# Hybrid decoder step on one core: the first head's operands turned inside the projection stage, the prompt's cross attention with the values held stationary, the last output tile half by half

## What is computed

```python
q = (_rms_norm(c_q, q_norm_g) @ w_uq).reshape(b, s, MLA_HEADS, NOPE_DIM + ROPE_DIM)
...
y_mla = _mla_prompt(q_lat, q_rope, c_kv, k_r, w_uv[l])          # 8 heads, causal, 1024 keys
mem_k, mem_v = _mem_kv(mem_prompt, w_mk[l], w_mv[l])            # 256 memory tokens
y_x = _cross_attention(q_x, mem_k, mem_v)                       # 4 heads of width 128
...
m = (g[:, :, 0] * ((y_mla * silu(z_mla)) @ w_p_mla) + ...)      # three gated branches
return _layer_norm(DEEPNORM_ALPHA * h + m @ w_o, ln_g, ln_b)
```

## Time and profile before

| | |
|---|---|
| median of 3 runs | 1564.25 us (1562.61 to 1572.33) |
| the profiled execution: own time, span | 1564.4 us, 1562.6 us |
| PE busy, share of the span | 1510.5 us, 97% |
| PEld busy | 1344.2 us, 86% |
| DVE, ACT, POOL busy | 663.3, 441.7, 411.4 us |
| mean granted clock of the tensor engine | 0.986 |

### The profile page before, as it was taken

One profiled execution on the slowest core, in us unless ns is written; L12 is line 12 of the kernel. 1 busy time (PEld: TensorE's weight loads), 2 busy tenths in 40 slices (PEclk: granted clock), 3 DMA queues, 4 the chain that ended last, 5 costly groups with the idle time before them and its releaser, 6 DMA issues.

```text
span 1562.6 us, 26122 instructions
## 1 busy us (share of the span) xinstructions
PE 1510.5 (97%) x10008; PEld 1344.2 (86%) x10008; DVE 663.3 (42%) x1451; ACT 441.7 (28%) x1066; POOL 411.4 (26%) x295
## 2 busy tenths in 40 slices
PE   7999999999999999978999999999999999999997
PEld 7998877775677777755999999999999999999885
DVE  3252367763533333334343452224533354019653
ACT  4223356661454444423111111111111121114100
POOL 3110057773023222101222222221222222226112
PEclk9999979999999999998999999999999999999998
DMA  5441020002643559447211211111121111113321
GB/s 208 142 190 33 4 78 1 1 1 75 176 122 106 157 165 236 138 143 253 49 41 41 54 42 41 47 49 41 41 54 42 47 40 49 41 42 108 109 95 54
DMA packets 104591, 131.25 MB, mean 84 GB/s; under 512 B 12338, under 2 KB 75634, under 8 KB 104468
## 3 DMA queue, kind: packets, MB, share of 16 engines
q1 hardware_dynamic: 102420, 125.39, 26.9%
q0 software_dynamic: 2048, 4.20, 1.1%
HBM read 113.84 MB, written 15.71 MB: 83 GB/s over the span
## 4 chain that ended last, share of the span: by engine, by line
PE 52%; issue 1%; DVE 0%; POOL 0%; POOLq 0%; ACT 0%
PE ps L1839 46%; PE ps L1863 6%; POOL p_h L1927 0%; POOLq L1768 0%; DVE p_stats L2081 0%; DVE p_h L2092 0%; DVE p_h L2077 0%; DVE p_h L2090 0%; PE ps L1850 0%; DVE p_mv L2084 0%; ACT p_rt L1909 0%; DVE p_rs L2088 0%; DVE p_ve L2086 0%
## 5 line engine op out<-in xcount | busy, mean ns | idle before, releaser
L1839 PE MATMUL ps<-p_xh,p_wh 128*128 128x352 f32 (+1 forms) x1152 | 377.5, 328 | 3.8 <-PEq L1543 3.8
L1839 PE MATMUL ps<-p_xh,p_wl 128*128 128x352 f32 (+1 forms) x1152 | 377.4, 328 | 0.0
L1839 PE MATMUL ps<-p_xl,p_wh 128*128 128x352 f32 (+1 forms) x1152 | 377.4, 328 | 0.0
L1917 POOL TENSOR_TENSOR p_wl<-p_wr,p_wh 128x512 fp32r<-128x512 f32 x116 | 162.2, 1414 | 519.2 <-DVE p_wh L1940 519.2
L1839 PEld LDWEIGHTS ps<-p_xh,p_wh 128*128 128x128 f32 x1152 | 217.1, 188 | 3.9 <-issue 3.9
L1839 PEld LDWEIGHTS ps<-p_xh,p_wl 128*128 128x128 f32 x1152 | 217.1, 188 | 0.0
L1839 PEld LDWEIGHTS ps<-p_xl,p_wh 128*128 128x128 f32 x1152 | 217.1, 188 | 0.0
L1940 DVE CAST p_wh<-p_wr 128x512 fp32r<-128x512 f32 x116 | 45.2, 425 | 340.3 <-ACT p_stage L1902 250.4
L1902 ACT ACTIVATE p_stage<-ps 128x384 f32<-128x384 f32 x168 | 79.5, 473 | 371.3 <-PE ps L1839 371.3
L833 POOL TENSOR_SCALAR p_pr<-p_pr,p_rec 128x896 f32<-128x896 f32 (+3 forms) x64 | 109.7, 1723 | 152.1 <-DVE p_rec L795 152.0
L874 POOL DMA_INDIRECT p_rawr<-cache_kr,p_rows x64 | 64.9, 1014 | 217.9 <-PE ps L1203 163.4
(11 more groups left out here) (291 smaller groups left out, 2669.5 us busy)
## 6 DMA issues: line engine op xcount, KB each, us to landing
p_rawc<-cache_ckv SPq DMA_DIRECT2D x256, 128.0 KB, 2.7
p_wr<-w_in SPq DMA_DIRECT2D x104, 256.0 KB, 2.9
x_kept<-p_xh SPq DMA_DIRECT2D x8, 544.0 KB, 6.6
x_kept<-p_xl SPq DMA_DIRECT2D x8, 544.0 KB, 6.7
p_xh<-x_kept SPq DMA_DIRECT2D x8, 544.0 KB, 4.2
p_xl<-x_kept SPq DMA_DIRECT2D x8, 544.0 KB, 4.2
p_xs<-x_prompt SPq DMA_DIRECT2D x8, 512.0 KB, 3.9
p_wr<-w_o SPq DMA_DIRECT2D x16, 256.0 KB, 2.8
```

The source lines that it names most:

```text
L1839: last = pe.matmul(ps[:, g % 8, 0:tn], w[:, v % HL, kt % UK, :], x[:, kt, t0:t0 + tn], start=(kt == 0 and q == 0), stop=(kt == nk - 1 and ...
L1917: nc.gpsimd.tensor_tensor(wl[:, v % HL], wr[:, v % RAW], f32(wh[:, v % HL]), ALU.subtract).then_inc(wl_done, 1)
```

## The change

There are three independent parts.

First head. `make_qkv` takes the sample tile first (`order`). At the end the products are rearranged (the values of a position come one step later), and the four turns of head 0, their copies and their subtractions are placed between the products of the last two positions. Their buffers lie elsewhere, so that `make_qkv` can write them. `prompt_attention` begins with scores.

Cross attention. The units are ordered so that four consecutive ones are one head and four row tiles. The probabilities are normalised on DVE before they are turned (`normed`), with four buffers in place of two and three places for scores. Two units' turned probabilities share a bank and one copy, and the product is done once for four units, the values stationary and 512 columns of probabilities moving. Its result has the layout of `y_x`, so the last turns are gone.

Output. For the last tile the first half's 24 products come before the second half's, and DVE does the residual and the statistics of a half when it is there. For all tiles, centring, scaling, gain and offset are two fused instructions on DVE in place of two on DVE and one on POOL; for the last tile they and the store are done by halves.

```diff
+
+
...
+    qh, ql = m("p3_qh", [QK, 2, SEQ], F32R), m("p3_ql", [QK, 2, SEQ], F32R)
+    kh, kl = m("p3_kh", [QK, 2, SEQ], F32R), m("p3_kl", [QK, 2, SEQ], F32R)
+    k["split"] = qh, ql, kh, kl
+    k["split_at"] = k["qkv_at"] + 2 * 4 * 2 * (QT + CT) * P
+    assert m.at <= k["top"] - 4 * 3 * P
...
         out = k["stored"][0]
         turned, ch_done, cl_done = sem("turned"), sem("ch_done"), sem("cl_done")
...
-                if i >= 2:
-                    pe.wait_ge(ch_done, i - 1)
-                    pe.wait_ge(cl_done, i - 1)
+            def turn(p):
...
+
+            def latent_part(p, j, done, kept):
+                if p > 1:
...
+            def head_turn(n):
+                part = HEAD_PARTS[n]
+                tiles = range(part % 2 * 4, part % 2 * 4 + 4)
+                if part < 2:
+                    pe.wait_ge(q_rope, 2 * (tiles[-1] + 2))
+                else:
+                    pe.wait_ge(k_rope, tiles[-1] + 1)
+                    pe.wait_ge(k_kept, tiles[-1] + 1)
...
+            for p in range(LAST):
+                turn(p + 1)
+                queries(p)
+                if p:
+                    latent_part(p, 0, k_done, k_kept)
+                if 0 < p < LAST - 1:
+                    latent_part(p, 1, v_done, v_kept)
+            head_turn(0)
+            head_turn(1)
+            queries(LAST)
+            latent_part(LAST, 0, k_done, k_kept)
+            latent_part(LAST - 1, 1, v_done, v_kept)
+            head_turn(2)
+            head_turn(3)
+            latent_part(LAST, 1, v_done, v_kept)
...
+            def head_high(n):
+                act.wait_ge(h_turned, n + 1)
+                src, high, _ = head_ends(n)
+                nc.scalar.activation(high, src, ACT.Copy).then_inc(h_high, 1)
...
+            for p in range(LAST):
+                hi(p + 1)
+                keep_q(p)
+                if p:
+                    keep_k(p)
+                if 0 < p < LAST - 1:
+                    keep_v(p)
+            head_high(0)
+            head_high(1)
+            keep_q(LAST)
+            keep_k(LAST)
+            keep_v(LAST - 1)
+            head_high(2)
+            head_high(3)
+            keep_v(LAST)
...
+            def head_low(n):
+                dve.wait_ge(h_high, n + 1)
+                src, high, low = head_ends(n)
+                dve.tensor_tensor(low, src, f32(high), ALU.subtract).then_inc(h_low, 1)
...
+            for p in range(LAST):
+                lo(p + 1)
+                rope(p)
+                if p:
+                    key_rope(order[p])
+            key_rope(order[LAST])
+            head_low(0)
+            head_low(1)
+            rope(LAST)
+            head_low(2)
+            head_low(3)
...
-    ring = [("turn", 0, part) for part in FIRST]
+    ring = []
...
-            for part in FIRST:
-                turn(("turn", 0, part))
...
+    PR = 4
+    pr, pt = m("p4_pr", [P, PR, MEM]), m("p4_pt", [P, 2, MT, BANK])
+    wukT, qsT = m("p5_wukT", [NOPE, H, KVL]), m("p5_qsT", [NOPE, H, NS])
+    nmax, tot, rec = m("p4_nmax", [P, PR]), m("p4_tot", [P, PR]), m("p4_rec", [P, PR])
     assert m.at <= k["dec_at"]
-    units = [(i, h) for i in range(NPT) for h in range(XH)]
+    units = [(4 * b + i, h) for b in range(NPT // 4) for h in range(XH) for i in range(4)]
...
+                if n >= 3:
+                    pe.wait_ge(exped, n - 2)
+                pe.matmul(ps[:, n % 3, 0:MEM], k["qx"][:, h, i * P:(i + 1) * P], kT[:, h, :],
+                          start=True, stop=True).then_inc(scored, 1)
...
+            def turn_probs(n):
+                pair = n // 2
+                pe.wait_ge(normed, n + 1)
+                if n % 2 == 0 and pair >= 2:
+                    pe.wait_ge(pt_done, pair - 1)
...
+                    last = pe.transpose(ps[:, 3 + pair % 2, j * 2 * P + n % 2 * P:j * 2 * P + (n % 2 + 1) * P],
+                                        pr[:, n % PR, j * P:(j + 1) * P], k["ident"][:, :])
+                last.then_inc(p_turned, 1)
+
+            def values(f):
+                _, h = units[4 * f]
+                pe.wait_ge(pt_done, 2 * f + 2)
+                if f >= 2:
+                    pe.wait_ge(y_kept, f - 1)
+                for j in range(MT):
+                    last = pe.matmul(ps[:, 5 + f % 2, :], mkv[:, 1, j, h * P:(h + 1) * P], pt[:, f % 2, j, :],
+                                     start=(j == 0), stop=(j == MT - 1))
                 last.then_inc(o_done, 1)
...
+            for n in range(NU + 5):
                 if n < NU:
...
+                    scores(n)
+                if 3 <= n < NU + 3:
+                    turn_probs(n - 3)
+                if n >= 8 and n % 4 == 0:
+                    values(n // 4 - 2)
...
+            def exp(n):
+                act.wait_ge(maxed, n + 1)
+                if n >= PR:
+                    act.wait_ge(p_turned, n - PR + 1)
+                    act.wait_ge(recd, n - PR + 1)
+                nc.scalar.activation(pr[:, n % PR, :], ps[:, n % 3, 0:MEM], ACT.Exp, bias=nmax[:, n % PR:n % PR + 1],
+                                     accum_out=tot[:, n % PR:n % PR + 1]).then_inc(exped, 1)
+
+            def keep_probs(pair):
+                f = pair // 2
+                act.wait_ge(p_turned, 2 * pair + 2)
+                if f >= 2:
+                    act.wait_ge(o_done, f - 1)
+                nc.scalar.activation(pt[:, f % 2, :, pair % 2 * 2 * P:(pair % 2 + 1) * 2 * P],
+                                     ps[:, 3 + pair % 2, :].rearrange("p (j w) -> p j w", w=2 * P),
+                                     ACT.Copy).then_inc(pt_done, 1)
+
+            def keep_y(f):
+                i, h = units[4 * f]
...
+                act.wait_ge(o_done, f + 1)
+                nc.scalar.activation(k["y_x"][:, h, i * P:i * P + BANK], ps[:, 5 + f % 2, :], ACT.Copy).then_inc(y_kept, 1)
...
+                    exp(n)
+                if n >= 4 and n % 2 == 0 and n - 4 < NU:
+                    keep_probs((n - 4) // 2)
+                if n >= 9 and n % 4 == 1:
+                    keep_y(n // 4 - 2)
...
-            for n in range(NU + 2):
...
-                if n >= 2:
...
+                if n:
+                    q = (n - 1) % PR
                     dve.wait_ge(exped, n)
-                    if n >= 3:
-                        dve.wait_ge(y_done, n - 2)
+                    if n > PR:
+                        dve.wait_ge(normed, n - PR)
                     dve.reciprocal(rec[:, q:q + 1], tot[:, q:q + 1]).then_inc(recd, 1)
+                    dve.wait_ge(recd, n)
+                    dve.tensor_scalar(pr[:, q, :], pr[:, q, :], rec[:, q:q + 1], None, ALU.mult).then_inc(normed, 1)
...
+                for cut in range(1 if i < NT - 1 else 2):
+                    cols = slice(0, D) if i < NT - 1 else slice(cut * BANK, (cut + 1) * BANK)
+                    sp.wait_ge(ready, i + cut + 1)
+                    sp.dma_start(x_src(i, "y_p", "y_s")[:, cols], hb[0:rows(i), i % 2, cols]).then_inc(out[i % 2], 16)
...
+                if i == NT - 1:
+
+                    for half in range(2):
+                        for t in range(KT):
+                            for q, (x, w) in enumerate(((mh, oh), (mh, ol), (ml, oh))):
+                                last = pe.matmul(ps[0:r, 2 * (i % 2) + half, :], x[:, t, i * P:i * P + r],
+                                                 w[:, t, half * BANK:(half + 1) * BANK],
...
-            pool.wait_ge(ln_in, 32)
-            for i in range(NT):
-                r = rows(i)
-                pool.wait_ge(scaled, i + 1)
-                nc.gpsimd.tensor_tensor(hb[0:r, i % 2, :], hb[0:r, i % 2, :], b_b[0:r, :], ALU.add).then_inc(ready, 1)
...
+                else:
+                    for half in range(2):
+                        cols = slice(half * BANK, (half + 1) * BANK)
+                        dve.wait_ge(o_done, i + 1 + half)
+                        dve.scalar_tensor_tensor(out=h[:, cols], in0=xr[0:r, s, cols], scalar=ALPHA,
+                                                 in1=ps[0:r, 2 * s + half, :], op0=ALU.mult, op1=ALU.add).then_inc(h_done, 1)
+                        dve.wait_ge(h_done, i + 1 + half)
+                        last = dve.bn_stats(stats[0:r, s, half, :], h[:, cols])
...
-                dve.tensor_scalar(h, h, mv[0:r, s, 0:1], one(rs), ALU.subtract, ALU.mult).then_inc(centred, 1)
-                dve.wait_ge(centred, i + 1)
-                dve.tensor_tensor(h, h, g_b[0:r, :], ALU.mult).then_inc(scaled, 1)
...
+                for cut in range(n_cut):
+                    cols = slice(cut * D // n_cut, (cut + 1) * D // n_cut)
...
+                    dve.scalar_tensor_tensor(out=h[:, cols], in0=h[:, cols], scalar=mv[0:r, s, 0:1], in1=g_b[0:r, cols],
+                                             op0=ALU.subtract, op1=ALU.mult).then_inc(scaled, 1)
+                    dve.wait_ge(scaled, i + cut + 1)
+                    dve.scalar_tensor_tensor(out=h[:, cols], in0=h[:, cols], scalar=one(rs), in1=b_b[0:r, cols],
```

(4 more changed lines are left out.)

242 lines of the change are left out of this document (95 added, 147 removed).

## The result

| | before | changed |
|---|---|---|
| median of 4 runs each, us | 1563.43 (1560.55 to 1572.33) | 1546.39 (1544.37 to 1548.82) |
| ratio, 95% interval | | 0.9889 (0.9861 to 0.9916) |
| profiled execution: own time, span | 1564.4, 1562.6 | 1548.82, 1547.0 |
| granted clock, mean | 0.986 | 0.992 |

A forecast was written before the change was run, and what follows sets the result against it. PE was taken to bound the kernel almost throughout, so time comes only from its idle, half-clock or removed work: 3.8 + 5.8 + 5.6 + 2.7 = 17.9 us off a 1562.6 span, forecast 1546.4 us, range 1542.5 to 1552.5.

The forecast's parts named there:

- Turns: End of `make_qkv`: head 0's turns move there, so the first score starts near 194.1 instead of 197.86; 3.8 us saved.
- The waits ahead of groups 3 and 4: `make_qkv`: PE's new waits before these groups of turns are covered by 12 products; without cover, some tenths.
- Clock: First head: at full clock, first score to turning of first probabilities takes 11.3 us instead of 16.8; 5.8 us saved in all.
- The clock stays: First head: PE idles about 1 us at the border, then has scores, so its granted clock stays full.
- the opposite: Rival: the clock falls anyway in the first head, 5.8 us less saved, 1552.2 us; chance 0.10.
- Cross: Cross attention: four units cycle in 4.96 us and the end goes; next block starts at 443.5 instead of 449.11, saving 5.6.
- the rival of 0.68: Cross loop: DVE's normalisation costs 0.68 us, or another wait of that size appears; 1549.3 us, chance 0.12.
- the floor by SP: Rival: shorter PE products let the cross loop run until SP's page transfers hold the border; 1543.4 us, chance 0.07.
- Tail: Behind the last product: DVE's halves gain 1.14 us and the fused instructions 1.55; together 2.7, range 2.2 to 3.2.
- the store of the last half is half as large; 0 to 0.3, I take 0: Tail: the smaller last store was put at a gain of 0 to 0.3 us and counted as 0.
- 1 to 2 us either way: Allowance for the clock moving in two short half-speed stretches at 704 and 722.
- The loss: Rival: the clock falls in the cross loop, 3.8 us more per four units, 1577 us if all eight; chance 0.03.

The follow-up runs named there:

- after_again: The changed kernel run once more, nothing altered; 1545.38 us, ratio 0.9887 to the kernel before.
- no_cross: The changed kernel with the old `cross_prompt`; 1554.31 us, ratio 0.9935 to the kernel before.
- no_tail: The changed kernel with the old `merge`; 1549.90 us, ratio 0.9911 to the kernel before.
- new_busy: The changed kernel with unread transposes where PE was idle between the attention and the merge; 1547.79 us, ratio 0.9873 to the kernel before.
- new_idle: The changed kernel with PE waiting for an unneeded DVE fill ahead of the first score; 1549.51 us, ratio 0.9914 to the kernel before.
- no_turns: The changed kernel with the old `make_qkv` and `prompt_attention`; 1554.33 us, ratio 0.9938 to the kernel before.
- act_order: The changed kernel; in the cross loop ACT copies turned probabilities ahead of the exponential, the last result behind both; 1547.98 us, ratio 0.9895 to the kernel before.
- act_order_pages: act_order with SP issuing 12 groups of pages in the cross attention instead of 16; 1545.47 us, ratio 0.9885 to the kernel before.
- all_busy: new_busy with the ACT order and 12 groups of pages of act_order_pages; 1543.84 us, ratio 0.9853 to the kernel before.
- old_busy_turns: The kernel before with only the 2, 3, 3, 3 unread transposes behind head 0's turns; 1565.35 us, ratio 0.9985 to the kernel before.
- old_busy: The kernel before with 18 unread transposes behind `make_qkv`'s last product and 2, 3, 3, 3 behind head 0's turns; 1560.02 us, ratio 0.9983.
- old_busy_border: The kernel before with only the 18 unread transposes behind `make_qkv`'s last product; 1563.37 us, ratio 0.9973 to the kernel before.

## Why the prediction was right

**Turns: 3.8 forecast, 4.3 measured.** The distance from the first PE instruction of `make_qkv` to the first score fell from 197.86 - 133.71 to 194.66 - 134.81. The table has only 3.2, because this execution entered the block 1.1 us later; the first score of the profiled executions that have the change lies between 193.59 and 196.06. The missing 0.5 is in three small terms: the wait for the first position's copy was 0.49 (0.6 forecast), four groups of turns 1.7 (2.0 taken), and the narrower first split saved 0.5 (PE's wait in front of its first product 0.82 instead of 1.32; 0.3 taken). The waits ahead of groups 3 and 4 never showed.

**Clock: 5.8 forecast, 5.72 measured**, and the rows 0.38, 1.07 and 0.28 of idle time (0.4, 1.3, 0.3 forecast) say that the walk was right as well. The 5.8 held 0.3 for the turning itself, which lies behind this stage; like for like it is 5.5 against 5.72. "The clock stays" is the weak step. The forecast gave the opposite 0.10 and named a fall after the border as a sign of being wrong, and such a fall came, in a weaker form: in four of the eight profiled executions that have the new turns and no added wait (after_again, no_cross, no_tail, new_busy) the clock falls right behind the second idle time, the 1.07 us before the fourth score, until about 204, and makes the stage 12.3 to 12.4 instead of 11.1. That the first trace had none is luck, worth 1.2 us. The Trainium skill, page "TensorE: Matmul & The Clock Gate", section "What's actually happening", says that the throttled state is the default and activity releases it, and I had held the measured 16.8 against it. new_idle's return, some 6 us behind the first score, is nearer to that than the 20 us of before and no_turns. The measured stages decide, and they have both lengths; for the sparse turns that this change removes it was the long one in both traces.

**Cross: 5.6 forecast, 6.09 measured.** The cycle was forecast as 4.96 and is 4.96; the normalisation costs 0.354 (0.33 taken), so the rival of 0.68 is out. The walk was right to 0.1 at every station (first `values` 6.98 us behind the first score, 6.9 forecast; last `values` 39.92, 39.9 forecast; the copy of its result over at 42.54, 42.5 forecast). What was mis-sized is the 0.5 added because the same walk of the old loop came out 0.5 short: the new loop had no such gap. act_order confirms the chain and act_order_pages the floor by SP, which in the forecast was a rival with 0.07: it binds only once the order on ACT is changed.

**Tail: 2.7 forecast, 3.31 measured.** Up to the issue it was 2.64. The step that failed in size is "the store of the last half is half as large; 0 to 0.3, I take 0": it gave 0.67, by landing 2.3 us after its issue instead of 2.9. The fused instruction costs 0.74 (0.7 taken). The product of two tensors before, in the same timeline as rows 10:

```profile
1555.58 1.22 DVE L2092 TENSOR_TENSOR p_h<-p_h,p_g 64x1024 f32<-64x1024 f32 x1
```

By the Trainium skill, page "VectorE: DVE Perf Modes", section "Why `tensor_tensor` can't do 2×_2P or 4×", a second tensor takes the read port that would fetch two elements of the first. The trace agrees in the times: 1024 columns take 0.80 us with one tensor, 1.22 with two, and 0.74 for each half when fused. Fusing still won, because four times 0.74 stand for 0.80 + 1.22 on DVE and 2.33 on POOL.

**Sum.** Forecast 17.9, by stages 4.3 + 5.72 + 6.09 + 3.31 = 19.4. The profiled execution has 15.6, as 1.1 were late ahead of the block and 2.7 came back in the two stages that hold the falls at 354 and 670; the median has 17.0. That 1546.4 was hit so closely is partly luck: the terms were 1.5 too small together, and 2.4 were lost elsewhere by the median, in the profiled execution mostly to new falls of the clock. The forecast had allowed "1 to 2 us either way" for clock changes, but at two other places, and those two falls stayed (at 691 and 709 now). The loss (0.03), a fall inside the cross loop, didn't occur in any trace; the turns were hidden.

## What to carry to other kernels

Cut two traces at the same few instructions and compare the stages: here that tells 0.1 us in the stages that neither a transfer nor the clock disturbs, where medians of four to twelve runs tell 3. Only the cut says whether a term was right or two errors met. An edit that removes a sparse stretch of the tensor engine is worth its idle time plus what the clock gives back behind it, and the second part can be priced on the old kernel alone, by unread transposes in the gap; the trace shows the full price (5.7 us here), the median how much of it is left over many runs (2.9). Where a loop's pace is a chain through one engine's queue, try the order in that queue, and look up the next floor first: here it was a third engine's transfers. The gain showed in the stage at once (2.7, then 4.06 us), in the median only in all_busy, where the clock was held.

## What the runs showed of the hardware

- The same idle time at the same place (2.0 us ahead of `cross_prompt`) was followed by a half-clock stretch in five profiled executions (changed, no_turns, no_cross, old_busy_turns, act_order_pages) and not in seven (before, after_again, no_tail, old_busy, old_busy_border, new_idle, act_order). One such fall made the stage 1.5 to 1.7 us longer. In no_cross, old_busy_turns and act_order_pages a second one followed 24 us later, and the stage is 3.1 to 3.4 longer.
- The spread of one kernel's times goes with its mean clock: the kernel before took 1560.7 and 1561.3 us at 0.990 and 1568.8 at 0.982 on one chip.
- The same code took 285.8 us up to the merge in old_busy and 290.1 in old_busy_border, both at the full clock in the decoding's first part, and the kernel before was 4.6 us slower on the chip of the second. All four profiled executions on that chip are 3.4 to 4.5 us longer in this stage than old_busy or after_again, with 1.3 to 1.6 us of PE waiting for ACT's `p_kT`. From the start of the stage to the transposes of `osum` some 233 us later, nine of the other executions agree within 0.05 us (232.84 to 232.89; act_order has 1.6 more by its fall), and the two fillings of the kernel before on this one have 236.92 and 237.02. Why that chip's decoding is slower stays open.
- A clock at half doesn't say how much time is lost: new_busy's mean clock is 0.998 against 0.993 of after_again, 0.005 of 1545 or 7 us of clock, and its time is 2.2 us less by the ratio.
